# Late RMS scale, a transposed state-space scan and a group-wise hand-over in a fused two-layer decoder step

## The reference, cut to what matters

```python
def rmsnorm(x, w): return x * rsqrt(mean(x * x) + EPS) * w
def swiglu(h, wg, wu, wd): return (silu(h @ wg) * (h @ wu)) @ wd
# layer 0: hybrid mixer (4 retention heads, 4 gated delta heads), then swiglu
# layer 1: Mamba-2 state space mixer (32 heads in 4 groups), then swiglu; a last rmsnorm
# state space, per chunk of tokens and head, with acs = cumsum(a):
y = einsum(cb, exp(acs_i - acs_j), x) + einsum(c, S) * exp(acs)
S = S * exp(acs_last) + einsum(b, exp(acs_last - acs), x)
y = y + x_conv * d;  y = y * silu(z);  y = y * rsqrt(mean(y * y) + EPS) * w;  out = y @ w_out
```

## Time and profile before

| what | us |
|---|---|
| median of three launches | 3383.99 (3383.58 to 3386.05) |
| profiled launch, own time | 3374.13 |
| its span, first to last instruction | 3372.3 |
| TensorE matmul busy | 3171.9 (94%) |
| weight loads busy | 3047.4 (90%) |
| VectorE busy | 1592.2 (47%) |
| GpSimd busy | 1006.2 (30%) |
| ScalarE busy | 782.3 (23%) |

### The profile page before, as it was taken

The page is one execution under the profiler, slowest core; times in us unless marked ns, Lnnn a source line. Parts: engine busy times, 40 slices in busy tenths (PEclk is TensorE's granted clock), DMA queues, the critical chain, the costliest instruction groups (busy, mean ns, idle before and its releaser), DMA issues.

```text
span 3372.3 us, 46391 instructions
## 1 busy us (share of the span) xinstructions
PE 3171.9 (94%) x20050; PEld 3047.4 (90%) x20050; DVE 1592.2 (47%) x1899; ACT 782.3 (23%) x1115; POOL 1006.2 (30%) x528
## 2 busy tenths in 40 slices
PE   6999899999799999999897999999978999999997
PEld 5999898888699999999887998989968999999997
DVE  5344647557632222221467858678686221222224
ACT  4222413414410000000134324143244100000002
POOL 2222211201023333332324535344441332333331
PEclk9999999999899999999999999999999999999998
DMA  4111100101011111111112223131220111111111
GB/s 144 65 64 59 53 26 26 46 26 33 20 50 44 51 44 50 44 44 51 39 43 94 79 78 108 57 107 66 88 91 27 53 49 46 44 51 44 51 44 63
DMA packets 79240, 190.79 MB, mean 57 GB/s; under 512 B 20900, under 2 KB 36932, under 8 KB 78920
## 3 DMA queue, kind: packets, MB, share of 16 engines
q1 hardware_dynamic: 52384, 150.03, 13.1%
q10 hardware_dynamic: 26664, 37.88, 3.5%
HBM read 164.07 MB, written 19.59 MB: 54 GB/s over the span
## 4 chain that ended last, share of the span: by engine, by line
PE 82%; DVE 11%; ACT 3%; issue 2%; DMA 1%; ACTq 0%; SPq 0%; DVEq 0%
PE ps_set L555 68%; PE ps_core L815 4%; PE ps_set L564 3%; ACT work L1073 2%; DVE work L1597 2%; PE ps_core L1010 2%; ACT L1073 1%; DVE work L1916 1%; DVE h_lo L1583 1%; PE ps_core L1015 1%; DVE work L1807 1%; DVE work L2127 1%; PE ps_core L1005 1%; DVE work L2079 1%; DMA x<-in_x 1%
## 5 line engine op out<-in xcount | busy, mean ns | idle before, releaser
L481 POOL CAST w_hi<-w_raw 128x1024 fp32r<-128x1024 f32 x230 | 260.0, 1130 | 2185.7 <-PE ps_set L555 1949.9
L555 PE MATMUL ps_set<-h_hi,w_hi 128*128 128x344 f32 x3696 | 812.5, 328 | 14.6 <-ACT work L1073 14.5
L555 PE MATMUL ps_set<-h_lo,w_hi 128*128 128x344 f32 x3696 | 784.5, 320 | 0.0
L555 PE MATMUL ps_set<-h_hi,w_lo 128*128 128x344 f32 x3696 | 780.9, 320 | 0.0
L555 PEld LDWEIGHTS ps_set<-h_hi,w_hi 128*128 128x128 f32 x3696 | 620.6, 188 | 37.7 <-issue 17.1
L555 PEld LDWEIGHTS ps_set<-h_lo,w_hi 128*128 128x128 f32 x3696 | 625.2, 189 | 0.0
L555 PEld LDWEIGHTS ps_set<-h_hi,w_lo 128*128 128x128 f32 x3696 | 616.7, 188 | 0.0
L484 POOL TENSOR_TENSOR w_lo<-w_raw,w_hi 128x1024 fp32r<-128x1024 f32 x230 | 597.8, 2599 | 18.4
L2014 DVE TENSOR_TENSOR work<-work,ps_set 128x1032 f32<-128x1032 f32 x44 | 54.1, 1229 | 816.2 <-PE ps_set L555 806.3
L1672 DVE TENSOR_TENSOR x<-x,ps_set 128x1032 f32<-128x1032 f32 x160 | 196.7, 1229 | 256.4 <-PE ps_set L555 256.4
L1073 ACT ACTIVATE work<-ps_set 128x1032 f32<-128x1032 f32 x116 | 120.1, 1035 | 721.5 <-PE ps_set L555 695.0
(11 more groups left out here) (224 smaller groups left out, 3427.8 us busy)
## 6 DMA issues: line engine op xcount, KB each, us to landing
w_raw<-in_w SPq DMA_DIRECT2D x230, 512.0 KB, 3.3
work<-ssm_cum_rows ACTq DMA_DIRECT2D x32, 512.0 KB, 4.1
sample<-in_ssm_state SPq DMA_DIRECT2D x16, 512.0 KB, 4.0
out_ssm_s<-sample SPq DMA_DIRECT2D x16, 512.0 KB, 2.6
x<-in_x SPq DMA_DIRECT2D x6, 688.0 KB, 14.8
work<-work ACTq DMA_DIRECT2D x16, 258.0 KB, 2.4
out_y<-x SPq DMA_DIRECT2D x6, 688.0 KB, 3.4
sample<-bc_rows SPq DMA_DIRECT2D x8, 512.0 KB, 4.8
```

Of the source, the lines that this page charges most:

```text
L481: return nc.gpsimd.tensor_copy(w_hi[:, k, :], w_raw[:, k, :])
L555: mm = nc.tensor.matmul(out[:, g, 0:TN], w[:, slot, cols], v[:, g * TN:(g + 1) * TN], start=(start and n == 0), stop=(stop and n == 2))
```

## The change

Five parts.

1. **Last gated delta head.** Its seven remaining filler slices leave the preparation and levels: one goes ahead of `u`, six into the first six steps of the scan, each with its addition on VectorE.
2. **Boundaries 1 and 3.** `h_hi` and `h_lo` are made from x times weight alone, without the root; the root, for all tokens at once (`RSTD`), is multiplied in behind the products: on VectorE, the gate tile out of PSUM by RSTD, `silu` on ScalarE in SBUF, the result by RSTD again, then by up. All outputs come first on TensorE, then projections and mean squares alternate.
3. **End of a feed-forward block.** The last up tile is done group by group, and gate-up product, `y_hi` and `y_lo` of tile B are made by group in every pair; the boundary's outputs of a group wait for that group alone.
4. **Scan.** `y` and `yc` are made with features on the partitions (x and the state are stationary now), so the four transposes and the copy into `yt` go. exp(acs) must then be a row along the tokens: two DMAs per chunk (64 partitions each) bring it from `ssm_cum_rows`, ScalarE exponentiates it, VectorE multiplies it by yc and later adds the product to the chunk.
5. **Last state space group.** One z slice instead of two behind the state update; the eight slices of the fourth z tile run after the scan, and its gate is multiplied in last.

Core of the diff (other parts only carry names and counts):

```diff
@@ boundary(n), TensorE
+                if n in (1, 3):
+                    for g in range(TG):
+                        outputs_of(g)
+                    projections(0)
+                    mean_square(0)
+                    projections(1)
+                    mean_square(1)
+                    projections(2, lambda: mean_square(2))   # between the two tiles
+                    return
@@ boundary(n), VectorE
+                def lows(g, first, last):
+                    ...
+                        v.scalar_tensor_tensor(h_lo[:, c, span(g)], x[:, c, span(g)], NORM_W[:, n, c:c + 1],
+                                               h_hi[:, c, span(g)].bitcast(F32), ALU.mult, ALU.subtract)
+                if n == 1:
+                    # all twelve adds, then
+                    lows(0, 0, KC); lows(1, 0, KC); sums(0); lows(2, 0, KC); sums(1); sums(2)
+                if n == 3:
+                    lows(0, 0, 4)
+                    for g in range(TG):
+                        add(g, 2)
+                        if g + 1 < TG:
+                            lows(g + 1, 0, 4)
+                        lows(g, 4, 6)
+                        add(g, 3)
+                        lows(g, 6, 8)
+                    for g in range(TG):
+                        sums(g)
@@ gated_delta, TensorE (late: last head)
-                fill(out, 1)
+                if h + 1 < HEADS:
+                    fill(out, 1)
...
+                fill(out, 0 if h + 1 == HEADS else 1)
...
+                if late:
+                    fill(out, 1)
                 pe.wait_ge(*gdn_dve.value(n("Nb")))
...
+                    if late and c < 6:
+                        fill(out, 1)
@@ ffn, VectorE
+                def gate(jobs, name, turn, unit, c, pair, before):
+                    ...
+                    v.tensor_tensor(grp(tok(c)), grp(RSTD), big(jobs.part(name)), ALU.mult)
+                    dve.wait_ge(*ffn_act[m].value("silu" + "AB"[c], pair))
+                    v.tensor_tensor(tok(c), tok(c), RSTD, ALU.mult)
@@ ffn_outputs, TensorE
+                pe.wait_ge(*ffn_dve[m].value(f"loB{g}", PAIRS - 1))
-                        pe.wait_ge(*ffn_dve[m].value("loB", PAIRS - 1))
@@ state_space, TensorE
-                        nc.tensor.matmul(ps_core[part][:, :], tok(5, c * P, c * P + P), work[:, 12, 0:512], ...)
+                        for t in range(4):
+                            mm = nc.tensor.matmul(ps_core[part][:, t * P:(t + 1) * P], work[:, 12, t * P:(t + 1) * P],
+                                                  tok(5, c * P, c * P + P), start=True, stop=True)
...
-                        mm = nc.tensor.matmul(ps_core[part][:, h * HD:(h + 1) * HD], SC_TILE[c % 2][:, h],
-                                              XDT[c % 2][:, h * HD:(h + 1) * HD], start=True, stop=True)
+                        mm = nc.tensor.matmul(ps_core[part][lower:lower + HD, h // 2 * P:(h // 2 + 1) * P],
+                                              XDT[c % 2][:, h * HD:(h + 1) * HD], SC_TILE[c % 2][:, h], start=True, stop=True)
...
-                    fill(z, 2)
-                    part = take(core, n(f"yt{c}"), 0, [n(f"y{c}")])
-                    for t in range(4):
-                        mm = nc.tensor.transpose(ps_core[part][:, t * P:(t + 1) * P], work[:, 11, t * P:(t + 1) * P], ident)
+                    fill(z, 2 if ahead else 1)
+                if not ahead:
+                    fill(z, KC)
@@ state_space, ScalarE, chunk c > 0
+                        end_rows(c, gr)          # two DMAs of 64 partitions x 4 x 128
                         differences(c, gr)
                         decays(c, gr)
+                        act.wait_ge(ecum_in[c % 2], ...)
+                        fn(ECUM[c % 2], ECUM[c % 2], ACT.Exp)
@@ state_space, VectorE: yt, its add and its copy go; the skip reads y in PSUM; new at the end of a chunk
+                        v.tensor_tensor(end, end, ps_core[core.part(n(f"yc{c}"))][:, :], ALU.mult)
+                        v.tensor_tensor(chunk, chunk, end.rearrange("p (t n) -> p t n", n=P), ALU.add)
```

More of the change, by code:

```diff
@@ L853, in gated_delta @@
                     mm.then_inc(*gdn_pe.step(n(f"X0{hf}")))
-                fill(out, 1)
+                fill(out, 0 if h + 1 == HEADS else 1)
+                late = h + 1 == HEADS
                 def decode(lv):
@@ L886, in gated_delta @@
                     if lv > 1:
-                        fill(out, 1)
+                        if not late:
+                            fill(out, 1)
                         decode(lv)
@@ L916, in gated_delta @@
                     fill(ahead, 2)
-                    if h + 1 == HEADS and c == 4:
+                    if late and c < 6:
+                        fill(out, 1)
+                    if late and c == 4:
                         gdn_rms(h, 0)
@@ L2016, in low @@
[L2016 to L2032 removed]
+                    if before is None:
+                        dve.wait_ge(*norm_act[2 * m + 1].value("rstd"))
+                    else:
+                        own(("loA", f"loB{TG - 1}")[c], before)
@@ new lines, in low_a, with gated_b, low @@
+                def low_a(pair):
+                    dve.wait_ge(*ffn_act[m].value("hiA", pair))
+                    v.tensor_tensor(y_lo[:, 0, :], tok(2), y_hi[:, 0, :].bitcast(F32), ALU.subtract).then_inc(*ffn_dve[m].step("loA"))
+                def gated_b(jobs, up, turn, unit, pair, last=False):
+                    def low(g):
+                        dve.wait_ge(*ffn_act[m].value(f"hiB{g}", pair))
+                        v.tensor_tensor(y_lo[:, 1, span(g)], tok(3)[:, span(g)], y_hi[:, 1, span(g)].bitcast(F32), ALU.subtract)\
+                            .then_inc(*ffn_dve[m].step(f"loB{g}"))
+                    own("fB", pair)
+                    for g in range(TG):
+                        if last and g < TG - 1:
+                            dve.wait_ge(part_done, parts + (PAIRS - 1) * 6 + g + 1)
+                        else:
+                            dve.wait_ge(unit_done, unit + 1)
+                        v.tensor_tensor(tok(3)[:, span(g)], tok(1)[:, span(g)], ps_set[jobs.part(up)][:, g, 0:TN], ALU.mult)\
+                            .then_inc(*((jobs.sem(up), 1) if g == TG - 1 else ffn_dve[m].step(f"gB{g}")))
+                        if g:
+                            low(g - 1)
+                    low(TG - 1)
@@ new lines, in pair @@
+                def pair(i, k, last=False):
+                    unit = i * 12 + (base + 4 + 6 * k)
+                    count = i * 2 + (k + 1)
+                    gate(loop, f"ga.{k}", i, unit, 0, count, i * 2 + k)
+                    gated_a(loop, f"ua.{k}", i, unit + 1, count)
+                    add_outputs(loop, [f"out{t}.{k}" for t in range(KC)], i, unit + 2, i * 12 + (parts + 6 * k))
+                    low_a(count)
+                    gate(loop, f"gb.{k}", i, unit + 4, 1, count, i * 2 + k)
+                    gated_b(loop, f"ub.{k}", i, unit + 5, count, last)
@@ L2163, in state_space @@
                     low(t)
+                    if t == 2 and gr + 1 == GROUPS:
+                        gate(3)
                 def scaled(t):
```

249 lines of the change are left out of this document (169 added, 80 removed).

## The result

The changed kernel takes **3363.6 us** (median of 4 launches, 3362.2 to 3369.3) against 3385.0 of the kernel before in the same series (3383.6 to 3386.2): ratio 0.9942, 95% interval [0.9931, 0.9954]. It is faster, by 21 us or 0.6%, which is clear of the noise; 57 were forecast and 3308 to 3352 was the range. The profiled launch of the changed kernel took 3362.2 us (span 3360.1), that of the kernel before 3374.1: 12 us apart.

A forecast was written before the change was run, and what follows sets the result against it. The scan was taken as bound by TensorE plus one handshake. Gains 0.8 + 12.0 + 9.7 + 13.0 + 15.6 + 6 = 57.1 us gave 3317.0 profiled and 3327 for the median, range 3308 to 3352.

The forecast's parts named there:

- rival A: Scan: VectorE binds it, gaining 0.2 us a chunk instead of 0.65; 3342 us in all, chance 0.2.
- rival B: Scan: y runs in two halves at once (1.0 us), gaining 28 us instead of 15.6; 3315 us, chance 0.08.
- Rival C: Scan: broadcast rows reach ScalarE late and slow the kernel; 3405 us for a landing of 7.5 us, chance 0.04.
- L: Scan: time a row broadcast takes to land; a chunk takes L + 4.3 us, deciding from 5.3 us on.
- the scan's bounds: Scan, groups 0 to 2: the gain forecast at 15.6 us could lie anywhere from 0 to 29 us.
- its stated bounds: Last gated delta head: -2 us if the additions hurt more, +3 if a slice also spares a clock fall.

The follow-up runs named there:

- e1: Changed kernel with GpSimd running all four sample-state rounds before the weight splits in the last state space group; 3350.5 us, ratio 0.9903.
- e2: Changed kernel with the fourth z tile's slices back in the last group's scan and its gate in the old place; 3352.7 us, ratio 0.9922.
- e14: Kernel of e2 with the low part of GpSimd's weight split in four quarters; 3347.8 us, ratio 0.9898.
- e6: Kernel before the change, three of four GpSimd operations per sample-state round cut to one sample of eight; 3373.4 us, ratio 0.9974.
- e5: Kernel of e1, three of four GpSimd operations per sample-state round cut to one sample of eight; 3314.0 us, ratio 0.9798.
- e7: Kernel of e1 with ScalarE issuing the next chunk's row broadcast before waiting for the carried rows; 3353.7 us, ratio 0.9913.
- e12: Kernel of e1 with the low part of GpSimd's weight split in four quarters, sample-state operations whole; 3348.8 us, ratio 0.9899.
- e15: Kernel of e12 with the last gated delta head's output products back in the levels, as before the change; 3346.1 us, ratio 0.9892.
- e4: Changed kernel run again unaltered; 3362.5 us.
- e9: Kernel of e1 with each GpSimd operation of the sample-state rounds issued as four quarter-size ones; 3376.1 us, ratio 0.9979.

## Why the prediction was wrong

**Part 5 (forecast +6, measured -10) is the step with the largest miss, 16 us.** The sentence that failed: "the state reduction of GpSimd comes no earlier", which took the fourth sample round to be there when VectorE wants it. VectorE waited 16.8 us for it; in the kernel before it waited for none of the sixteen. Slices that move in TensorE's program move every release of a weight slot; GpSimd's split of the next tile waits for that slot, and a sample round stood behind the split. e1 returned 12 us. What is left is no gain (64.8 + 25.5 us in e1 against 70.2 + 20.6). The prediction did name VectorE as the limit of this scan, at 8.9 us a chunk; the seven chunks took 9.3 each without the slices (e1) and 9.1 with them (e2), so the slices cost nothing where they were (e2, e14).

**Part 4 (forecast +15.6 in groups 0 to 2, measured +4.6) has a wrong size in the scans, by rival A's mechanism, and a term put at nothing behind them.** The three scans took 67.5, 67.2 and 64.6 us, 70.1 before: 11 us gained of 15.6. The stages from the sum to the next group took 112.7 to 114.5 us, 111.1 before: 6.6 us lost, where the sum had no term.

In the scans TensorE's side went better than forecast. In the chunks from 2027 to 2043 of the changed kernel, which no gate and no hold disturbed, a chunk takes 8.0 us, not 9.2, since the 16 matmul records of `y` end 1.09 us after the first one starts (nearer to rival B; in the kernel before 1.89 by the same measure):

```profile
2030.41 1.09 PE L1055 MATMUL ps_core<-work 128*64 128x128 f32 x16
```

What was mis-sized is VectorE's time, and in it the addition within SBUF, put at 0.85 us: L2308 had a mean of 1.40 in group 1 (8.4 us in six) and 2.8 where it met GpSimd. The mean of another operation with two SBUF inputs in the old scan (1.02) was taken as the upper end of one that falls at another moment. Behind it all of VectorE's queue moved, and it became the bound: TensorE now waits 26.2 us for L2235 (14 times) where it had waited 24.0 for the skip. The same cut of GpSimd's work gives 36 us to the new kernel and 10 to the old, so it is the new one that pays for GpSimd: from e6 to e5 the change, with the order of e1, gains 59 us. With TensorE waiting, its granted clock in the scans was 0.95, 0.95, 0.97 and 0.89, where it had been 1.00; what that costs was not separated.

Behind the scans two waits are new. VectorE waits for the fourth sample round (3.1 us on average in groups 0 to 2 of the changed kernel, nothing before), and TensorE waits 1.8 to 2.1 us for ScalarE. In e5 both are gone and the stage takes 110.5 us, so the loss comes with GpSimd's rounds; the chain from one to the other was not followed.

Rival C did not occur: ScalarE waited for landings (3.9 us in two waits in group 1), but e7 was worth nothing. (By the prediction's own numbers C decides from L = 9.3 - 4.3 = 5.0 us on, not 5.3, and the range holds all of the scan's bounds; neither changes the forecast.)

**Part 2 (12.0 and 9.7, measured 9.1 and 4.8).** The mechanism was right. At boundary 3 the missing 4.9 us are additions held by the weight split (seven take 10.8 us, 7.7 in e12, while the `lows` take 14.5 and 15.0; e12's stage is 56.1, a gain of 7.4 over the earlier trace rows), and the clock, 0.89 for the 15 us in which TensorE waits 2.4 us for a bank and 2.4 for the first sum. The 58.7 us were a quick launch: with the same code there the other profiles have 60.2 to 60.4, a gain of 3.2. At boundary 1 the stall behind the first outputs stayed, as forecast (4.6 us, clock 0.75 in the first 16.7 us). The size that was off is `lows`: 0.57 us each undisturbed and 0.66 in the mean, priced at 0.52, the time of the old operation (0.51), with two waits of TensorE for them (1.7 and 1.8). The first sum began 33.5 us behind the first output instead of 30.9, which is 2.6 of the 2.9 missing.

**Part 3 (6.5 each, measured 4.5 and 4.9).** The stall went and the clock behind it is 1.00, as forecast; 96 matmuls took 16.8 us instead of 15.1, with a wait of 1.3 us for an addition among them. The prediction named the split of the second output tile as the next to be late. It was there in time for TensorE, but while it ran (1647.07, 2.55 us) it held VectorE's low parts for 2.7 us, and behind these stood the addition that frees a bank.

**Part 1 (+0.8, measured -1.4; 0.5 lost by e15)**: within its stated bounds, the levels giving 8.0 instead of 9.3 and the scan losing 9.2 instead of 8.5, its steps growing to 3.65 us (3.66 forecast).

**The FFN blocks** were right: 4464 matmuls, no wait for the 44 added operations per block, although half of these are held to 2.26 us each (median; 1.8 was the most that the forecast allowed).

**The base.** 9.9 us between the profiled launch of before and its median were carried over; for the changed kernel that difference is 1.4. e4 (5.8 us above its median) and e6 (2.1 above) show that it is spread, not a property of the program. This helped the forecast by 8.5 us: against the profiled launches the miss is 45 us, against the medians 36.6.

## What to carry to other kernels

When an operation on VectorE changes from one SBUF and one PSUM input to two SBUF inputs, do not price it by its size: look at what GpSimd does at that moment, because here every one of the 168 that began while a two-input GpSimd operation had over 0.1 us left ended after it (0.68 us became 2.82). When slices move on TensorE, follow every buffer that they release through the producers' programs, and see what else those producers have behind that wait. Where one engine leaves the critical path, ask which one is next (VectorE was busy for 59.0 of 67.2 us), and test it by moving work of the first: if nothing moves (e2), it was not the bound. And when a stretch gets shorter, look at what others finish in its shadow: the fourth sample round was ready in time only as long as the scan took 70 us.

## What the runs showed of the hardware

- The changed kernel's `y` (L1055: 64 stationary and 128 moving columns, neighbouring heads written to different halves of the output partitions) has its records start in pairs, in all 32 chunks at most 0.02 us apart. The 16 records end in 1.09 us in the 25 chunks where the clock is 1.00 meanwhile, and in 1.78 to 1.98 in the seven where it is 0.50 to 0.57. The old `y` with 128 stationary and 64 moving columns took 1.89 in 26 of 32, and 16 records with 128 and 128 took 2.05. Whether the width or the alternation does it, no run separates.
- VectorE and GpSimd held each other. In the trace of the changed kernel the VectorE operation with two SBUF inputs that began second ended after the GpSimd one in 168 of 168 cases for two-input operations and in 27 of 33 for the CAST. GpSimd's two-input operations of 1024 columns take 2.34 to 2.41 us alone (L495, L527, L529; L520 and L524 take 1.90) and up to 3.6 when they begin during a VectorE operation with two SBUF inputs, its CAST 1.04 to 1.07 and up to 2.0. Small copies on VectorE, with one input, were held too: L1941 (128x8) took 0.16 to 0.17 us alone and 2.36 to 2.38 in each of the 15 cases beside a two-input operation.
- A two-input GpSimd operation of 256 columns takes 0.88 us on average in the sample rounds of e9 (L496), against 2.87 for one of 1024 in e1 (L529), and 0.95 in the weight split of e12 against 2.6 in e1 (L495): four pieces cost 23% and 44% more.
- The two DMAs per chunk with pieces of 128 columns (L1524), issued from ScalarE's queue, occupied it for 0.6 us each (median 0.61 and 0.62), against 0.33 for the one of whole rows (L1515).
